# Last iteration of a mixture-of-experts kernel: weight chunks in smaller pieces, the second transposes inside the down-projection, the last sums behind the branch

## The reference

```
h2     = rms_norm(x, norm2_g)
gates  = softmax of the 4 largest of 32 router logits (h2 @ router_w + router_b)
for each expert e and each token that chose it:
    hc  = h2 @ w_in[e] + b_in[e]                 # 1024 -> 2 * 1024 (glu, lin)
    act = min(glu, 7) * sigmoid(1.702 * min(glu, 7)) * (clip(lin, -7, 7) + 1)
    y   = act @ w_out[e] + b_out[e]              # 1024 -> 1024
out    = x + sum over the token's experts of gate * y
```

## Time and profile before

| what | value |
|---|---|
| median of 3 runs | 1085.4 us (1083.84 to 1086.44) |
| the profiled execution | 1084.59 us |
| its span in the profile | 1082.8 us |
| PE busy | 973.3 us (90%) |
| DVE, ACT, POOL busy | 239.7, 141.3, 35.4 us |
| mean granted clock of PE | 0.976 |
| HBM read | 423.48 MB |

### The profile page before, as it was taken

One profiled execution on the slowest core, in us unless ns is written; L12 is line 12 of the kernel. 1 busy time (PEld: TensorE's weight loads), 2 busy tenths in 40 slices (PEclk: granted clock), 3 DMA queues, 4 the chain that ended last, 5 costly groups with the idle time before them and its releaser, 6 DMA issues.

```text
span 1082.8 us, 11807 instructions
## 1 busy us (share of the span) xinstructions
PE 973.3 (90%) x4852; PEld 429.6 (40%) x4853; DVE 239.7 (22%) x476; ACT 141.3 (13%) x246; POOL 35.4 (3%) x37
## 2 busy tenths in 40 slices
PE   7898989999998899789988999789988998899887
PEld 5786553433332334233433343233423343334332
DVE  4676261112111202012101210120201210121011
ACT  5476140000000001010000000000101000000000
POOL 3720000000000000000000000000000000000000
PEclk9899989999999999999999999999999999999999
DMA  8646968899999999999999999999999999999994
GB/s 271 189 159 231 432 266 354 345 431 426 427 428 428 427 429 429 429 427 429 429 430 427 429 429 429 427 429 428 430 427 429 428 430 427 427 428 430 425 422 181
DMA packets 41138, 424.94 MB, mean 392 GB/s; under 512 B 5806, under 2 KB 7892, under 8 KB 15924
## 3 DMA queue, kind: packets, MB, share of 16 engines
q1 hardware_dynamic: 41092, 424.53, 93.9%
q10 hardware_dynamic: 16, 0.00, 0.0%
HBM read 423.48 MB, written 1.05 MB: 392 GB/s over the span
## 4 chain that ended last, share of the span: by engine, by line
DMA 53%; PE 39%; SPq 2%; ACT 2%; DVE 2%; issue 1%; DVEq 0%; ACTq 0%
DMA ring<-in_moe_w_in_dram 34%; PE bank L1305 18%; DMA ring<-in_moe_w_out_dram 17%; PE bank L1347 10%; PE bank L1038 3%; PE bank L1176 3%; DMA ring<-in_w_in_dram 2%; PE bank L1381 2%; PE bank L1243 1%; SPq L306 1%; ACT split_parts L484 1%; PE bank L1321 0%; PE bank L1282 0%; DVE acc L979 0%; SPq L323 0%
## 5 line engine op out<-in xcount | busy, mean ns | idle before, releaser
L1305 PE MATMUL bank<-ring,area 128*64 128x512 f32 x2016 | 453.1, 606 | 50.1 <-DMA ring<-in_moe_w_in_dram 48.5
L1305 PEld LDWEIGHTS bank<-ring,area 128*64 128x64 f32 x2016 | 154.1, 140 | 340.8 <-issue 338.4
L1347 PE MATMUL bank<-ring,area 128*64 128x512 f32 x1024 | 228.5, 601 | 12.1 <-DMA ring<-in_moe_w_out_dram 11.6
L1347 PEld LDWEIGHTS bank<-ring,area 128*64 128x64 f32 x1024 | 77.3, 138 | 154.3 <-issue 152.7
L963 DVE TENSOR_SCALAR area<-bank 128x512 f32<-128x512 f32 x32 | 22.0, 686 | 467.2 <-PE bank L1305 467.2
L979 DVE TENSOR_TENSOR acc<-bank,acc 128x512 f32<-128x512 f32 x64 | 39.8, 684 | 284.6 <-PE bank L1381 284.6
L649 ACT ACTIVATE area<-bank 128x512 f32<-128x512 f32 x32 | 19.1, 597 | 581.1 <-PE bank L1305 581.1
L1038 PE MATMUL bank<-split_parts 128*128 128x512 f32 x288 | 73.8, 419 | 5.9 <-DVE split_parts L685 5.5
L1038 PEld LDWEIGHTS bank<-split_parts 128*128 128x128 f32 x288 | 58.4, 205 | 19.0 <-DVE split_parts L685 3.2
L1381 PE MATMUL bank<-area 128*128 128x512 f32 x128 | 59.2, 605 | 0.0
L1243 PE MATMUL bank<-area 128*128 128x128 bf16 x768 | 46.6, 221 | 12.4 <-DVE area L947 12.4
(11 more groups left out here) (188 smaller groups left out, 351.7 us busy)
## 6 DMA issues: line engine op xcount, KB each, us to landing
ring<-in_moe_w_in_dram SPq DMA_DIRECT2D x124, 2048.0 KB, 26.9
ring<-in_moe_w_out_dram SPq DMA_DIRECT2D x62, 2048.0 KB, 24.8
ring<-in_w_in_dram SPq DMA_DIRECT2D x5, 2048.0 KB, 13.4
ring<-in_w_out_dram SPq DMA_DIRECT2D x2, 2048.0 KB, 8.3
area<-in_moe_w_in_dram SPq DMA_DIRECT2D x2, 2048.0 KB, 8.4
ring<-in_moe_w_in_dram SPq DMA_DIRECT2D x4, 1024.0 KB, 28.1
ring<-in_moe_w_out_dram SPq DMA_DIRECT2D x4, 1024.0 KB, 27.8
ring<-in_w_in_dram SPq DMA_DIRECT2D x4, 512.0 KB, 7.2
```

Of the source, the lines that this page charges most:

```text
L1305: ins = pe.matmul(bank[n][64 * e:64 * e + 64, :], xeT[a][:, k, 64 * e:64 * e + 64], chunk(c + e, first)[:, f:f + GROUP], start=False, stop ...
L1347: ins = pe.matmul(bank[6 + dh][64 * e:64 * e + 64, :], actT[:, k, 64 * e:64 * e + 64], ring[:, (c + e) % RING, f:f + GROUP], start=False, ...
```

## The change

- Chunks 16 to 21 of the last iteration are issued in halves, 22 and 23 in quarters (`PIECES` takes the place of `HALVED`). SP issues a pair piece by piece, c and c+1 in turn, after both of its slots are free. Every piece but a chunk's last has its own semaphore, and PE waits for the pieces that hold row k right before row k (`row_arrived`), in the up-projection and in the down-projection. The order "column half outermost" is dropped.
- In every job `turn` is cut in two: the first half's transposes and the gates' come before `down`, the second half's are issued inside `down`, before k = 2. ACT copies the gates' transposes before the second half.
- On DVE the last `combine` moves from iteration 7 to behind the branch, into the Else part (and into the If part, when rounds follow). In every job the first add waits for one spreading matmul instead of two.
- `drain` with `result_ready`, and SP's wait for it with its stores, move into the If part. In the case without further rounds SP does neither and has no second flag load and branch.

```diff
-HALVED = (JOB_CHUNKS + IN_CHUNKS - 2, JOB_CHUNKS + IN_CHUNKS - 1, 2 * JOB_CHUNKS - 2, 2 * JOB_CHUNKS - 1)
+PIECES = {c: 2 for c in range(JOB_CHUNKS + IN_CHUNKS - 4, 2 * JOB_CHUNKS - 2)}
+PIECES.update({2 * JOB_CHUNKS - 2: 4, 2 * JOB_CHUNKS - 1: 4})
...
+                if last:
+                    last(True)
                 done = eng.alloc_register("iterations_done")
...
+                if more:
+                    more()
+                eng.nop()
             with eng.Else():
-                if no_more:
-                    no_more()
+                if last:
+                    last(False)
...
-                if half is not None:
-                    cols = slice(half * CHUNK_F // 2, (half + 1) * CHUNK_F // 2)
+                if piece is not None:
+                    width = CHUNK_F // PIECES[c]
+                    cols = slice(piece * width, (piece + 1) * width)
...
-                    if static(it, ITERS - 1) and c in HALVED:
+                    if static(it, ITERS - 1) and c in PIECES:
                         if c % 2 == 0:
                             sp.wait_ge(chunks_used, it * ITER_CHUNKS + c - RING + 2)
-                            for half in range(2):
-                                fill_half(c % RING, quad, c, half)
-                                fill_half((c + 1) % RING, quad, c + 1, half)
+                            for i in range(PIECES[c]):
+                                fill_piece(c % RING, quad, c, i)
+                                fill_piece((c + 1) % RING, quad, c + 1, i)
...
-            all_rounds(sp, run, store_after_round_0)
-            sp.wait_ge(result_ready, 1)
-            with sp.If(sp.value_load(flags[0:1, 24:25], min_val=0, max_val=1) != 0):
+            def store_result():
+                sp.wait_ge(result_ready, 1)
                 for n in range(4):
                     store(n)
-            with sp.Else():
-                sp.nop()
+
+            all_rounds(sp, run, store_sums, store_result)
             sp.wait_ge(out_stored, 16 * 4)
...
-                    act.wait_ge(gatherT_psum, j + 1)
-                    act.activation(gatherT, bank[0][:, 0:S], ACT.Copy).then_inc(gatherT_ready, 1)
+                        if hf == 0:
+                            act.wait_ge(gatherT_psum, j + 1)
+                            act.activation(gatherT, bank[0][:, 0:S], ACT.Copy).then_inc(gatherT_ready, 1)
...
-                    dve.wait_ge(comb_psum, 3 * j + max(n, 1))
+                    if n:
+                        dve.wait_ge(comb_psum, 3 * j + n)
+                    else:
+                        dve.wait_ge(chunks_used, JOB_CHUNKS * (j + 1))
...
-                combine(j + 1)
-
-            all_rounds(dve, run)
-            dve.drain().then_inc(result_ready, 1)
+                if not static(it, ITERS - 1):
+                    combine(j + 1)
+
+            def last_sums(more_follows):
+                combine(PAIRS * ITERS - 1)
+
+            def tell_result():
+                dve.drain().then_inc(result_ready, 1)
+
+            all_rounds(dve, run, last_sums, tell_result)
...
+            def row_arrived(it, c, b, count):
+
+                pieces = PIECES[c] if static(it, ITERS - 1) and c in PIECES else 1
+                if b * pieces % count:
+                    return
+                i = b * pieces // count
+                if i < pieces - 1:
+                    pe.wait_ge(piece_full[c][i], 16)
                 else:
                     arrived(it, c, static(it, 0))
...
-                for rows in range(2):
-                    c = a * JOB_CHUNKS + IN_CHUNKS + 2 * rows
-                    pe.wait_ge(hiddenT_ready, 2 * j + 1 + rows)
+                for k in range(KD):
+                    rows, b = divmod(k, ROWS_OUT)
+                    if b == 0:
+                        pe.wait_ge(hiddenT_ready, 2 * j + 1 + rows)
+                    if k == 2:
+                        turn(j, a, 1)
                     for e in range(2):
-                        half_arrived(it, c + e)
...
+                        row_arrived(it, a * JOB_CHUNKS + IN_CHUNKS + 2 * rows + e, b, ROWS_OUT)
+                    for dh in range(2):
+                        slice_of(k, dh)
...
-                turn(j, 0, first)
+                if not first:
+                    pe.wait_ge(comb_added, 4 * j)
+                turn(j, 0, 0)
+                turn_gates(j, 0)
                 out_bias(j, 0)
...
-                turn(j + 1, 1, False)
+                turn(j + 1, 1, 0)
+                turn_gates(j + 1, 1)
                 down(it, j + 1, 1, False)
```

More of the change, by code:

```diff
@@ L197, in build @@
         ring_full = [sem(f"ring_full{s}") for s in range(RING)]
-        half_full = {c: sem(f"half_full{c}") for c in HALVED}
+        piece_full = {c: [sem(f"piece_full{c}_{i}") for i in range(PIECES[c] - 1)] for c in PIECES}
         result_ready = sem("result_ready")
@@ L246, in flag_column, with all_rounds @@
             return (rnd - 1) * ITERS + quad
-        def all_rounds(eng, run, no_more=None):
+        def all_rounds(eng, run, last=None, more=None):
             run(0, 0, 0)
@@ L287, in load_group, with fill @@
                     .then_inc(w_in_full[g], 16)
-            def fill(buf, full, quad, c, half=None):
+            def fill(buf, full, quad, c, piece=None):
                 job, r = divmod(c, JOB_CHUNKS)
@@ L309, in fill_ring, with fill_piece @@
                 fill(ring[:, slot, :], ring_full[slot], quad, c)
-            def fill_half(slot, quad, c, half):
-                fill(ring[:, slot, :], ring_full[slot] if half else half_full[c], quad, c, half)
+            def fill_piece(slot, quad, c, i):
+                fill(ring[:, slot, :], ring_full[slot] if i == PIECES[c] - 1 else piece_full[c][i], quad, c, i)
             def fill_extra(i):
@@ L397, in store, with store_sums @@
                 sp.dma_start(out[0, t * P:(t + 1) * P, cols], acc[:, t, cols]).then_inc(out_stored, 16)
-            def store_after_round_0():
-                for n in range(4):
+            def store_sums(more_follows):
+                for n in range(0 if more_follows else 4):
                     sp.wait_ge(comb_added, 4 * PAIRS * ITERS - 3 + n)
                     store(n)
-            all_rounds(sp, run, store_after_round_0)
-            sp.wait_ge(result_ready, 1)
-            with sp.If(sp.value_load(flags[0:1, 24:25], min_val=0, max_val=1) != 0):
+            def store_result():
+                sp.wait_ge(result_ready, 1)
                 for n in range(4):
                     store(n)
-            with sp.Else():
-                sp.nop()
+            all_rounds(sp, run, store_sums, store_result)
             sp.wait_ge(out_stored, 16 * 4)
@@ L1253, in chunk @@
                 return extra[c - FIRST_EXTRA] if first and FIRST_EXTRA <= c < RING else ring[:, c % RING, :]
-            def half_arrived(it, c):
-                if static(it, ITERS - 1) and c in HALVED:
-                    pe.wait_ge(half_full[c], 16)
+            def row_arrived(it, c, b, count):
[5 more added lines that the diff above has]
+                    pe.wait_ge(piece_full[c][i], 16)
                 else:
@@ L1297, in up @@
                     for e in range(2):
-                        if b == 0:
-                            half_arrived(it, c + e)
-                        elif static(it, ITERS - 1) and c in HALVED:
-                            arrived(it, c + e, False)
+                        row_arrived(it, c + e, b, ROWS_IN)
                     for n in (0, 2, 1, 3):
@@ L1312, in up, with turn, turn_gates @@
                             ins.then_inc(hidden_psum, 1)
-            def turn(j, a, first):
-                if not first:
-                    pe.wait_ge(comb_added, 4 * j)
-                for hf in range(2):
-                    pe.wait_ge(hidden_ready, 2 * j + hf + 1)
-                    for i in range(4):
-                        ins = pe.transpose(bank[4 + hf][:, i * P:(i + 1) * P], act_t[:, hf, i::ROWS_OUT], ident[:, :])
-                        if a == 1 and hf == 0 and i == 0:
-                            ins.then_inc(chunks_used, 1)
-                    ins.then_inc(hiddenT_psum, 1)
+            def turn(j, a, hf):
+                pe.wait_ge(hidden_ready, 2 * j + hf + 1)
+                for i in range(4):
+                    ins = pe.transpose(bank[4 + hf][:, i * P:(i + 1) * P], act_t[:, hf, i::ROWS_OUT], ident[:, :])
+                    if a == 1 and hf == 0 and i == 0:
+                        ins.then_inc(chunks_used, 1)
+                ins.then_inc(hiddenT_psum, 1)
+            def turn_gates(j, a):
                 pe.wait_ge(gated_ready, j + 1)
@@ L1354, in slice_of @@
                         ins.then_inc(y_psum, 1)
-                for rows in range(2):
-                    c = a * JOB_CHUNKS + IN_CHUNKS + 2 * rows
-                    pe.wait_ge(hiddenT_ready, 2 * j + 1 + rows)
-                    for e in range(2):
-                        half_arrived(it, c + e)
```

(19 more changed lines are left out.)

## The result

| | us |
|---|---|
| changed kernel, median of 4 runs | 1077.59 (1077.04 to 1079.73) |
| kernel before, median of 4 runs beside it | 1084.62 (1083.25 to 1086.44) |
| ratio | 0.9938, 95% interval 0.9916 to 0.9959 |
| profiled execution, its span | 1079.73, 1078.0 |

The forecast was 1079.3 us, a ratio of 0.9944. Two later comparisons of the same two kernels, with 12 and 35 runs each, gave 0.9974 (0.9961 to 0.9986) and 0.9968 (0.9955 to 0.9982): a gain of about 3 us, not 6 or 7. The profiled execution was the slowest of the four, so its span understates the first comparison's gain.

A forecast was written before the change was run, and what follows sets the result against it. Expert weights streaming at 427 GB/s bound the kernel, leaving only its end to win. Gains of 3.95 and 2.2 sum to 6.15 us: execution 1084.59 to 1078.4, median 0.8 above, 1079.3 us; range 1077.2 to 1082.6.

The forecast's parts named there:

- Rival D: Rival, chance 0.05: up-projection and hand-over stay as late as now, pieces gain nothing; tail or nothing, 1083.2 to 1085.4 us.
- A: Rival, 0.15: late clock fall, 1079.9 to 1080.8 us. As distance: iteration 0's first spreading matmul to last weights' landing.
- E: Rival, chance 0.04: pacing by pieces keeps the clock at half through the down-projection; slower, 1093 us.
- B: Rival, 0.12: tail gives half or nothing, 1080.3 to 1081.5 us. As distance: last weights' landing to down-projection's end.
- C: Rival, 0.08: pieces cost transfer time, 1080.4 to 1082.7 us. As distance: down-projection's end to span's end.
- One sign that I had named for being wrong: At the last weights: the forecast is wrong if the last piece lands after 1068.5 us; 1067.4 was expected.
- Steps 1 to 3: Last job: halved chunks, transposes inside the down-projection, quartered last pair; down-projection ends at 1069.3 against 1073.25, 3.95 us gained.
- The price of small pieces: Last chunks' transfer: halves and quarters cost 0, the good bound; bad bound 1.1 us at the stores' rate.
- Step 2: Hand-over: second transposes inside the down-projection let it start 2.1 us behind the up-projection, at 1053.4; part of 3.95 us.
- Step 4: SP's issues: 20 instead of 12, covered by 25 to 31 us to landing; cost nothing, without cover 3.4 us.
- Step 5: Transposes moved in all 16 jobs: PE's waits between 215 and 1030 us take them up; cost and gain 0.
- Step 6: Tail: last sums behind DVE's branch, SP only closing; 7.35 us instead of 9.55, gain 2.2, bounds 1.2 and 0.

The follow-up runs named there:

- after_again: Changed kernel repeated without edit, as yardstick; ratio 0.9974 to the kernel before.
- first_whole: Changed kernel with chunks 16, 17, 20 and 21 whole again, 18 and 19 in halves, 22 and 23 in quarters; ratio 1.0000 to the kernel before.
- all_whole: Changed kernel with every chunk whole, 22 and 23 included; ratio 1.0016 to the kernel before.
- last_in_halves: Changed kernel with chunks 22 and 23 in halves instead of quarters; ratio 0.9982 to the kernel before.
- turn_back: Changed kernel with the second half's transposes and the gates' copy back in front of the down-projection in all jobs; ratio 0.9959 to the kernel before.
- tail_alone: Kernel before with the tail's edit alone: last sums behind DVE's branch, SP without the second load; ratio 0.9984 to the kernel before.
- turn_alone: Kernel before with the moved transposes alone; ratio 1.0009 to the kernel before.

## Why the prediction was right, and where its steps failed

**Direction, bound and range.** Faster, as forecast, and 1077.6 us lies within the range. The end is set by the last landing, with PE waiting for it, and by SP's closing steps: both as in the forecast. Rival D needed PE late and was not seen; A and E needed a clock at half behind the hand-over, and the changed kernel shows none. B came true only by 0.25 us (7.6 for 7.35), C by about 0.5. One sign that I had named for being wrong did appear: the last piece landed after 1068.5, at 1068.6, and at 1069.2 in after_again. It pointed at what failed, the landings.

**Step by step**, with the mean of the three profiles of the changed kernel against the one of before:
- *Steps 1 to 3, the way to the down-projection's end, 3.95 us.* From iteration 0's spreading it is 866.4 before and 863.7 after: 2.7. B gained 3.85, from 5.9 to 2.0, nearly as said; A lost 1.0, about half by the pieces and half by the early branch. The up-projection's end (1051.9 for 1051.3), the hand-over (2.0 for 2.1) and the place of the transposes were right. I took 14.18 us, twice 7.09, for 64 records at full clock; they take 13.95 (first_whole, iteration 0), so the two falls of the clock in the kernel before cost 1.5 and 1.7 us, not 1.3 and 1.5.
- *The price of small pieces, taken as 0, bad bound 1.1.* This term failed: all_whole, the kernels with four halved chunks and those with all pieces show 860.2, 860.6 to 861.2 and 861.2 to 861.8; with the branch in the same place that is 0.5 more than before, half of the bad bound. The nearest row, a 2 MB load with rows of 4 KB, could not show it: its 8.3 us are the middle of two loads of 7.6 and 9.0, and 3.4 of them are beyond the 4.9 that 2 MB take in the stream. The rule of the Trainium skill ("DMA: Bandwidth & Descriptors", Bandwidth), at least 1 MiB per DMA, pointed the right way. My estimate by it was too dear: 3.3 us for the quarters alone, where quarters in place of halves show 0.2 in last_in_halves. Which property of a piece costs, its row length or one more issue, is open.
- *Step 2 by itself* gained nothing: turn_back ends as early. The landings would have said so, since k=7 had to wait for the last quarter with either hand-over.
- *Step 4, SP,* at nothing: held issues of over 2 us did not reach the landing.
- *Step 5, the same move in 16 jobs, at 0.* This failed. I took the waits between 215 and 1030 us for the slack of all jobs, but iteration 0 lies ahead of 215 us, where the DMA share is not yet full and PE paces the transfers. There it costs 0.8 us, of which 0.6 to 0.8 arrive at the last landing.
- *Step 6, the tail, 2.2 us*: C fell from 9.6 to 7.6, so 2.0, and 1.7 by the time of tail_alone. Its reason held: the 3.5 us from DVE's branch to its next instruction are 0.7 of it by themselves, SP's wait for DVE and its second load the rest. What it left out is that the early branch makes the landing 0.5 us later, so that 1.7 net remain.
- *Rival E's price*, 1093, is the end of the span; as a median, by the sum's own step, it would have been 1096.

**Sum by what was measured:** 2.7 + 2.0 - 0.8 = 3.9 us, a ratio of 0.9964, inside the intervals of the two long comparisons and just outside that of the first. The forecast's 6.15 is outside those two. So the forecast had the mechanism and overstated it by more than half of what was measured, for three costs at zero: the pieces (0.5), the early branch (0.5) and the first job of iteration 0 (0.8); that the first comparison came out beside it is, by the longer ones, partly luck.

## What to carry to other kernels

In a kernel bound by a stream of transfers, look for the stretch where the stream is not yet full: a delay of 0.8 us in that stretch was paid nearly in full at the end here, while 2 us saved just ahead of the last landing may be worth nothing. Price pieces by the whole stream's length with and without them, not by a single load. And when a branch skips a long body, put it where its engine has nothing to do, and let nobody wait for that engine behind it; then look whether the last transfers land later for it.

## What the runs showed that I had not expected

- The distance A is the same within 0.6 us in the ten profiles of kernels with quarters or more halves, though its start varied from 205.8 to 208.4 us: what moves it in these runs is the size of the pieces and the place of DVE's branch, by about 0.5 us each.
- Matmuls of 64 columns take 0.22 us a record while PE has work for both experts (3.65 us for 16) and about 0.43 when it has work for one alone. The Trainium skill ("TensorEngine Tiling (Array Packing)", Key Properties) says that different tiles work independently and in parallel; the trace agrees, by the factor of two.
- A wait of 2.7 us for chunk 16 brought the clock to half in the kernel before (64 records in 15.48 us) and in tail_alone (15.40), and not in first_whole and turn_alone (13.95, after waits of 2.73 and 2.71 us). In all_whole it stayed at 1.00 behind a wait of 2.71 us for chunk 16 and fell behind the next one, for 18:

```profile
1047.00 8.48 PE L1320 MATMUL bank<-ring,area 128*64 128x512 f32 x32 [2.70 <-DMA ring<-in_moe_w_in_dram]
```

Behind the gaps of 4 us in first_whole and turn_alone and the hand-over of turn_back it fell each time. So the same gap cost nothing or 1.4 to 1.5 us in these profiles, and they do not show what decides.
